# Per-bank completion signals in a three-block network's token-major projections

## The reference, cut to what matters

```
even:  qa,fa,ia,ga,qb,kb,vb = split(h @ w_in)     # HGRN2 scan with values ia, stick-breaking attention with values vb
odd:   qk,v,og,gates       = split(h @ w_in)     # conv + SiLU on qk, mLSTM scan with values v, output gate og
attn:  qa,ka,va,qb,ckv,... = split(h @ w_in_2)   # dilated windows with values va, latent top-k attention
each:  x = x + gate * (mixed @ w_out);  x = x + gate * ffn(norm(x))
```

## Time and profile before

| | before |
|---|---|
| time, median of 3 runs | 1964.46 us |
| time of the profiled run | 1965.65 us |
| its span, first to last instruction | 1963.8 us |
| TensorE busy | 1915.9 us (98%) |
| POOL busy | 1195.5 us (61%) |
| VectorE busy | 1038.4 us (53%) |
| ScalarE busy | 452.0 us (23%) |
| mean granted TensorE clock | 0.987 |

### The profile page before, as it was taken

The page is one execution under the profiler, slowest core; times in us unless marked ns, Lnnn a source line. Parts: engine busy times, 40 slices in busy tenths (PEclk is TensorE's granted clock), DMA queues, the critical chain, the costliest instruction groups (busy, mean ns, idle before and its releaser), DMA issues.

```text
span 1963.8 us, 25238 instructions
## 1 busy us (share of the span) xinstructions
PE 1915.9 (98%) x8828; PEld 1548.2 (79%) x8828; DVE 1038.4 (53%) x1539; ACT 452.0 (23%) x779; POOL 1195.5 (61%) x915
## 2 busy tenths in 40 slices
PE   6999999999999999999999999999999999999998
PEld 5787868888888887666888888888776788888887
DVE  7566267766654544456666654224788552323222
ACT  3302341212120022253212111013228321111000
POOL 3743326778876965423688887775552456666773
PEclk7999999999999999999999999999999999999999
DMA  7532223455554532211355554332220123223332
GB/s 306 182 118 76 97 84 119 163 188 199 190 200 173 182 104 86 64 44 32 118 213 193 190 194 141 105 115 89 78 73 23 34 86 100 98 97 98 99 107 75
DMA packets 67376, 242.24 MB, mean 123 GB/s; under 512 B 7498, under 2 KB 7882, under 8 KB 67314
## 3 DMA queue, kind: packets, MB, share of 16 engines
q1 hardware_dynamic: 65536, 237.01, 34.7%
q10 hardware_dynamic: 1778, 4.37, 0.6%
HBM read 239.25 MB, written 2.10 MB: 123 GB/s over the span
## 4 chain that ended last, share of the span: by engine, by line
PE 91%; DVE 4%; ACT 2%; DMA 2%; issue 1%; POOL 1%; SPq 0%; DVEq 0%; ACTq 0%; POOLq 0%
PE gemm L474 22%; PE gemm L475 22%; PE gemm L476 22%; PE gemm L528 2%; PE gemm L529 2%; PE gemm L501 2%; PE gemm L503 2%; PE gemm L502 2%; PE gemm L513 2%; DMA w_raw<-wstream 2%; PE mix L701 1%; PE gemm L854 1%; DVE sq_acc L1417 1%; PE mix L474 1%; PE mix L475 1%
## 5 line engine op out<-in xcount | busy, mean ns | idle before, releaser
L439 POOL TENSOR_TENSOR w_lo<-w_raw,w_hi 128x1024 fp32r<-128x1024 f32 x302 | 743.8, 2463 | 25.2
L474 PE MATMUL gemm<-h_hi,w_hi 128*128 128x512 f32 x1448 | 566.2, 391 | 3.9 <-POOL w_lo L439 3.1
L476 PE MATMUL gemm<-h_hi,w_lo 128*128 128x512 f32 x1448 | 564.3, 390 | 0.0
L475 PE MATMUL gemm<-h_lo,w_hi 128*128 128x512 f32 x1448 | 564.1, 390 | 0.0
L436 POOL TENSOR_TENSOR pool_gate<-pool_gate 128x1 f32<-128x1 f32 x298 | 108.5, 364 | 643.3 <-PE gemm L476 339.5
L437 POOL TENSOR_SCALAR w_hi<-w_raw 128x1024 fp32r<-128x1024 f32 x302 | 345.3, 1144 | 16.9 <-DMA w_raw<-wstream 16.9
L474 PEld LDWEIGHTS gemm<-h_hi,w_hi 128*128 128x128 f32 x1448 | 272.3, 188 | 61.4 <-POOL w_lo L439 3.5
L476 PEld LDWEIGHTS gemm<-h_hi,w_lo 128*128 128x128 f32 x1448 | 272.2, 188 | 56.8
L475 PEld LDWEIGHTS gemm<-h_lo,w_hi 128*128 128x128 f32 x1448 | 272.3, 188 | 55.8
L1128 DVE CUSTOM_DVE_ANT_0 ada_raw<-ada_raw,c_act 128x1024 f32<-128x1024 f32 x128 | 213.3, 1683 | 104.5 <-DMA ada_raw<-adastream 104.5
L476 PE MATMUL gemm<-p_hi,w_lo 128*128 128x512 f32 x528 | 205.4, 389 | 0.0
(11 more groups left out here) (352 smaller groups left out, 2264.2 us busy)
## 6 DMA issues: line engine op xcount, KB each, us to landing
w_raw<-wstream SPq DMA_DIRECT2D x302, 512.0 KB, 3.5
ada_raw<-adastream SPq DMA_DIRECT2D x128, 512.0 KB, 4.3
a_early<-adastream SPq DMA_DIRECT2D x8, 1024.0 KB, 11.7
out<-x_res SPq DMA_DIRECT2D x8, 256.0 KB, 2.2
x_res<-x_in SPq DMA_DIRECT2D x2, 512.0 KB, 6.3
c_act<-c_in ACTq DMA_DIRECT2D x2, 512.0 KB, 7.1
x_res<-x_in ACTq DMA_DIRECT2D x2, 512.0 KB, 9.0
b_dist<-const_in ACTq DMA_DIRECT2D x1, 512.0 KB
```

The source lines that it names most:

```text
L439: pool.tensor_tensor(wlo[s][:], raw[:, u % RAW, :], whi[s][:].bitcast(F32), ALU.subtract).then_inc(w_split, 1)
L474: pe.matmul(out_ap, w_h, r_h, start=first, stop=False)
L475: pe.matmul(out_ap, w_h, r_l, start=False, stop=False)
L476: return pe.matmul(out_ap, w_l, r_h, start=False, stop=last)
```

## The change

The bank signals: in the last chunk of each body the last matmul of banks 0, 1 and 2 increments a new semaphore `token_banks`. ScalarE waits for that before it copies banks 0 to 2, and for `pe_done` only before bank 3. The odd layer's hardware loop becomes two written-out passes, and the attention layer's copies go in the order 0, 1, 2, 3. In the even layer ScalarE's four AO8 copies (`between_blocks(8)`) move ahead of the second body's four bank copies.

```
@@ token_body
                             mm = pe.matmul(G[j][:], b, wh, start=False, stop=(k == KT - 1))
+                        if u == 3 and j < NTB - 1:
+                            mm.then_inc(sig("token_banks"), 1)
                     mm.then_inc(pe_done, 1)
@@ tokens
-                act.wait_ge(pe_done, N0["even_in"] + c)
                 for j in range(4):
+                    if j < 3:
+                        act.wait_ge(sig("token_banks"), 3 * i + j + 1)
+                    else:
+                        act.wait_ge(pe_done, N0["even_in"] + c)
                     act.activation(VT[:, i, j, :], G[j][:], ACT.Copy).then_inc(gfree[j], 1)
@@ after the Silu of the output gate
+            between_blocks(8)
             tokens(1, 20)
-            between_blocks(8)
             between_blocks(9)
@@ odd layer
-            with act.Fori(0, 2) as i:
-                act.wait_ge(pe_done, 4 * i + N0["odd_in"] + 12)
+            for i in range(2):
                 for j in range(4):
-                    act.activation(OV[:, j, ds(512 * i, 512)], G[j][:], ACT.Copy).then_inc(gfree[j], 1)
+                    if j < 3:
+                        act.wait_ge(sig("token_banks"), 6 + 3 * i + j + 1)
+                    else:
+                        act.wait_ge(pe_done, 4 * i + N0["odd_in"] + 12)
+                    act.activation(OV[:, j, 512 * i:512 * i + 512], G[j][:], ACT.Copy).then_inc(gfree[j], 1)
@@ attention layer
-            act.wait_ge(pe_done, N0["attn_in"] + 12)
-            for j in (3, 0, 1, 2):
+            for j in range(4):
+                if j < 3:
+                    act.wait_ge(sig("token_banks"), 12 + j + 1)
+                else:
+                    act.wait_ge(pe_done, N0["attn_in"] + 12)
                 act.activation(VA[:, j, :], G[j][:], ACT.Copy).then_inc(gfree[j], 1)
```

## The result

The changed kernel takes 1951.94 us, the median of 5 runs (1949.98 to 1955.01), against 1962.74 us for 5 runs of the kernel before beside it (1961.06 to 1967.02). The ratio is 0.9944, with a 95% interval of 0.993 to 0.9958. The forecast was 1954.9 us, faster by more than 0.3%, in a range of 1951.0 to 1960.5. The measured time lies in the range, and faster was right. The time itself came out 3.0 us under the forecast, nearly all of it because the forecast was taken off the profiled run (1965.65 us) and the 5 runs of the kernel before have a median 2.9 us lower. The two medians differ by 10.8 us and the forecast sum was 10.73; so close a match is partly luck, since the interval allows 8.2 to 13.7 us and the two profiled runs differ by 13.9.

The account below looks back on a forecast made before the run. TensorE was taken to bound the kernel, so only its waits pay: 6.08 us of stalls plus 4.65 us of clock, 10.73 us off the profiled 1965.65, gave 1954.9 us, range 1951.0 to 1960.5.

Parts of the forecast that it names:

- The stalls: Four TensorE waits on ScalarE copies, at token-major body ends and before level 9, would go: 6.08 us.
- Body 1 and level 9: Stall after the first even body goes whole, -0.94 us; wait before scan level 9 goes by copying AO8 first, -2.74 us.
- the step between the odd bodies: TensorE's matmul-to-matmul step between the two odd_in bodies, 1.17 us, would shrink to a steady 0.23: -0.94 us.
- The stall before the first scores: After the second odd body, only the fourth bank copy would still delay the first mLSTM scores: -1.46 us.
- The cover: Early copies finish in time: AO8 with 0.5 us to spare, odd bank 0 2.2 us early; attention gains 0 us.
- Levels 2 and 3: Even layer's scan after body 1: VectorE's chain of levels 2 to 8 moves forward with level 2's matmuls, no cost.
- The increments: Fifteen body matmuls get a semaphore increment: 0, or at most 0.15 us; the Trainium skill's page would give 0.4 us.
- The clock at level 9: Level 9's 16 matmuls would run at full instead of half clock once the idle before them goes: 1.58 us.
- Rival (b): No clock comes back at level 9 or head 0; only the stalls are gained: 1959.6 us, chance 0.11.
- The clock in head 0: First mLSTM head would run at full clock, 8.81 us instead of 11.88: 3.07 us gained.
- rival (a): Stalls go, but mLSTM head 0 stays at the lower clock because of its small matmuls: 1958.0 us, chance 0.22.
- Rival (d): Slower: the clock falls at norm borders between phases, 3.07 us each; 1974.9 us if five fell, chance 0.02.

Follow-up runs that it names:

- body1_late: Changed kernel, but the copies of the even layer's first token-major body wait for the last bank again: 1953.62 us, ratio to the kernel before 0.9945.
- odd_only: Kernel before plus bank signals used in the odd layer alone; even and attention layers copy as before: 1961.01 us, ratio 0.9977.
- scores3: Changed kernel, but the first mLSTM scores wait for three bank copies, the fourth wait standing before the first values: 1952.58 us, ratio to the kernel before 0.9942.
- scores3_warm: Changed kernel with first scores waiting for three bank copies, plus three idle-filling matmuls ahead of norm border 3's first wait: 1951.86 us, ratio to before 0.9937.
- signals_only: Changed kernel with the AO8 copies back behind the second even body's bank copies, so bank signals alone: 1954.59 us, ratio to the kernel before 0.9946.
- before_again: Kernel before, unchanged, executed once more for one profile: 1960.37 us in that single execution.
- swap_only: Kernel before with only the four AO8 copies moved ahead of the second even body's bank copies, no bank signals: 1957.41 us, ratio 0.9966.

## Why the prediction was right, and where its numbers were off

**The stalls** were forecast at 6.08 us and are 6.29. Body 1 and level 9 were exact, and so was the step between the odd bodies (1.17 us before, 0.23 now). Behind it come 0.11 us that the forecast left out: after the idle the second matmul starts 0.34 us after the first (778.51 to 778.85), not 0.23. I had priced a stall by the step across it alone; after body 1 there are 0.13 us of the same kind, which stand in the row of levels 2 and 3.

The stall before the first scores is 0.10 us larger than forecast for another reason. ScalarE began its copies 0.52 us after the start of the last L503 there, and does so 0.43 us after it now (793.88 to 794.31). The kernel before has a register instruction of the hardware loop between the end of the wait and each copy (engine ACTq, its sequencer):

```profile
L2045 ACTq FUSED_REGOPS  x8: 46/46/52, 777.8 to 800.9; - x8
L2045 ACT ACTIVATE o_v<-gemm x8: 592/600/616, 777.9 to 802.2; 128x512 f32 x8
```

After each odd body its first one starts 0.42 us after L503, where a copy without the loop starts, and the copy follows 0.10 us later. I had booked this work at zero because ScalarE idles there; it idles before the wait ends, and the register instruction comes after. Unrolling without the signals was not tried.

**The cover** behaved as said. AO8 ends before level 9 asks for it, L1341 comes in time, bank 0 of the odd body is copied from 768.67, long before the next body at 772.35, and the attention layer's ScalarE is early only to wait 2.81 us for VectorE instead of 1.34. There the shift doesn't change.

**Levels 2 and 3** are a step that I had wrong: I wrote that VectorE's chain moves forward with the matmuls, at no cost. It does, but against POOL, whose splits follow TensorE by other steps: VectorE's product of level 2 takes 1.65 us instead of 1.25. The matmuls of chunk 12 had won 0.13 us, so net of that 0.26 of the 0.94 us is given back. body1_late shows that it belongs to the earlier start. The modulation sum behind level 1 also meets POOL (L1141, 1.02 us instead of 0.16), but VectorE idles 1.88 us after it, so it delays nothing.

**The increments** cost nothing that can be seen, and nothing of the 0.4 us that the prediction gave as the other estimate. In the last chunk of body 1 the 24 matmuls take 5.34 us from the first start to the last in before, changed and odd_only, and in both odd bodies and in attention 5.21 us in all three, with the increments and without. Line L503 of the changed kernel, answering to the earlier trace rows:

```profile
L503 PE MATMUL gemm<-w_hi,h_lo x160: 388/389/397, 86.3 to 1432.6; 128*128 128x512 f32 x160
```

**The clock at level 9** was forecast at 1.58 us and is 1.76: I priced 16 matmuls at full clock at 3.44 us, and they take 3.27. The mechanism stands: the four profiles with the wait of 2.6 us have the stretch, and the eight without it or with 1.05 us don't (five of the table, body1_late, scores3 and scores3_warm). Rival (b), no clock back, falls in every profile. The rule of the Trainium skill ("TensorE: Matmul & The Clock Gate", on why this matters for kernels) that rival (b) leaned on warns only of longer idle gaps; by it these 2.58 us would have been harmless, and the four profiles say otherwise.

**The clock in head 0** was forecast at 3.07 us and is 3.12, and head 0 takes the 8.81 us that I had worked out. But rival (a) is half alive: signals_only and odd_only have no wait there and still one stretch of 3.4 us, which costs 1.5 us. The changed kernel and its variants have none in six profiles (the three above, body1_late, scores3, scores3_warm). Filling the wait removes the stretch as well as removing it does. So the idle is a cause, and it is not the only one; what the second is was not settled. The 3.07 us were one term with one cause in the forecast; two of eight profiles without the wait still pay half of it, so that it came whole in the profiled run was partly luck.

**What I had not forecast** are the other 3.1 us of the first pair of profiles (13.87 against 10.73). All but 0.2 of them is clock elsewhere: 1.49 us near 903 and 3.04 at 954 gained, 1.64 at 1309 lost. They can't be booked to the change: the kernel before, executed again, differs from itself by 5.28 us in the same pieces. I had said that such stretches come and go and had left room for one; there are two kinds of such drift. One is the clock. The other, which does not enter the first pair but the later ones, is TensorE's wait for VectorE at norm border 3, 1.49 us, which has another cause (below). Whether the change also shifts how often they come isn't known: the medians differ by 10.8 and 13.7 us in the two comparisons, and the sum of the repeating pieces, 10.9, lies in both intervals. Rival (d) is seen in one place, the new stretch at 1309 us, 1.64 us, in two of three profiles of the changed kernel, in four of six with its variants, and in none of the other six.

## What to carry to other kernels

When a group of accumulators completes one after the other, signal each one, and put ahead of it in the consumer's queue whatever is ready sooner: here the order of two groups of copies was worth 4.5 us and needed no signal. Price a stall of TensorE from start to start, and add what the matmuls behind it lose if the granted clock there is 0.50; a stall that can't be removed can be filled (one profile shows it, at the scores; the times don't). Before a difference of a few microseconds is explained, profile the same kernel twice and compare the two, since everything that differs between them is not the edit's.

## What the runs showed of the hardware

**VectorE stands still behind POOL.** L1417 adds two tiles of 128x512 in SBUF, always the same work. The timeline of the kernel before:

```profile
937.71 2.40 POOL L439 TENSOR_TENSOR w_lo<-w_raw,w_hi 128x1024 fp32r<-128x1024 f32 x1
937.86 2.79 DVE L1417 TENSOR_TENSOR sq_acc<-sq_acc,sq_tile 128x512 f32<-128x512 f32 x1 [0.70 <-ACT sq_tile L1970]
```

and that of before_again, where it once starts ahead of the split:

```profile
937.21 0.76 DVE L1417 TENSOR_TENSOR sq_acc<-sq_acc,sq_tile 128x512 f32<-128x512 f32 x1 [0.70 <-ACT sq_tile L1970]
937.51 2.71 POOL L439 TENSOR_TENSOR w_lo<-w_raw,w_hi 128x1024 fp32r<-128x1024 f32 x1
```

Started 0.15 us after POOL's, it ends 0.54 us after POOL's end and takes 2.79 us; started 0.30 us ahead, it takes 0.76, and POOL's takes 2.71 instead of 2.40. The first case renews itself: add, L1146 and the square on ScalarE make 4.1 us, one chunk of TensorE, so VectorE meets the next split just after its start again, seven times in a row, and TensorE waits 1.33 us for it at norm border 3. If it slips out of step once, that wait is gone, which the table of pieces counts as 1.49 us: in the table of profiles it stands in five of nine, in before and not in before_again, which are the same kernel. The stretches at half clock at border 3 stand only where this wait is (four of the five), so the two go together, though it wasn't tried apart: scores3_warm, which fills that wait, was never seen with it. The Trainium skill, "SBUF — State Buffer", section on the two separate sides, says that a VectorE operation with two SBUF inputs and a GpSimd operation that reads SBUF exclude each other for the whole instruction; these rows agree, 2.79 against 0.76 us. The 1.65 us of L1340 above is the same.

**The granted clock** fell to 0.50 after 1.67 us of idle among small matmuls, between 1.1 and 1.7 us after the end of the idle, three times of three (before, before_again, swap_only); it stayed at 1.00 when that idle was filled, and after 1.05 us of idle before level 9. The length of the idle alone doesn't decide. In the attention layer TensorE waits 1.69 us (until 1480.65) and 2.02 us (until 1532.30) for ScalarE before L1068, between matmuls of 128 columns, and the clock stays at 1.00. The same two waits stand in all twelve profiles, and none has a stretch at half clock there. TensorE's waits from 1475 to 1540 us of the kernel before (in total, times, longest):

```profile
PE gemm L1068 <- ACT b_pt L2193: 5.7, 8, 2.0
```

and stretches of it (the column before the DMA share is the clock):

```profile
1478.00:1486.00 8.00, 6.31 (x56) 4.29 (x57) 6.77 (x23) 7.19 (x22) 1.16 (x2) 1.00 0.21 66
1530.00:1538.00 8.00, 5.56 (x51) 3.66 (x49) 1.24 (x3) 4.92 (x12) 0.62 (x1) 1.00 0.00 0
```

And an idle of 3.08 us that ends near 62 us has a stretch at half clock beginning during it or within 1.2 us of its end in eight of the twelve profiles; of three profiles of the changed kernel, one has it. So the falls that followed each time at level 9 and at the scores are what these executions show, not a rule for idle of that length. A stretch of 3.4 us costs 1.4 to 1.8 us, one of 6.8 us 2.8 to 3.1.
